# Update and norm between two stages by halves of the tokens, in a two-layer diffusion block on one core

## The reference

```python
def rms_norm(x, g):
    y = xf * lax.rsqrt(jnp.mean(xf * xf, axis=-1, keepdims=True) + EPS)
def modulate(x, g, shift, scale):
    return rms_norm(x, g) * (1.0 + scale) + shift
def swiglu(u, wg, wu, wd):
    return (jax.nn.silu(u @ wg) * (u @ wu)) @ wd
def ffn_sublayer(x, shift, scale, gate, g_pre, g_post, wg, wu, wd):
    y = swiglu(modulate(x, g_pre, shift, scale), wg, wu, wd)
    return x + FFN_RES * gate * rms_norm(y, g_post)
...
h = ffn_sublayer(h, ...); hc = ffn_sublayer(hc, ...)                # latent, context
y, yc = token_mixing(modulate(h, ...), modulate(hc, ...), ...)      # w_in 1024 x 2608, attention, gla, mLSTM, w_out
h = h + mod[:, 5] * rms_norm(y, g[3])
h = ffn_sublayer(h, ...)
if need_ctx: hc = ...                                               # not in the last layer
```

## Time and profile before

| | us |
|---|---|
| median of 3 runs | 1999.89 (1999.27 to 2004.18) |
| profiled execution | 2008.94 |
| its span, first to last instruction | 2007.1 |
| PE busy in it | 1873.5 (93%) |
| DVE busy | 1109.3 (55%) |
| ACT busy | 760.1 (38%) |
| POOL busy | 243.6 (12%) |

### The profile page before, as it was taken

One profiled execution on the slowest core, in us unless ns is written; L12 is line 12 of the kernel. 1 busy time (PEld: TensorE's weight loads), 2 busy tenths in 40 slices (PEclk: granted clock), 3 DMA queues, 4 the chain that ended last, 5 costly groups with the idle time before them and its releaser, 6 DMA issues. The chain is left out here.

```text
span 2007.1 us, 25666 instructions
## 1 busy us (share of the span) xinstructions
PE 1873.5 (93%) x10461; PEld 1521.9 (76%) x10461; DVE 1109.3 (55%) x1630; ACT 760.1 (38%) x1132; POOL 243.6 (12%) x327
## 2 busy tenths in 40 slices
PE   5999999979998886999999979999999799879998
PEld 3788877857786664888778858887888488769997
DVE  1777722245756646777522267775222676855544
ACT  4423222236436445222313253222232645654443
POOL 4011110012531000111110001110000152000000
PEclk7999999989999797999999979999999799979999
DMA  9566654342321022666553416665234243036654
...
DMA packets 366469, 254.05 MB, mean 127 GB/s; under 512 B 30610, under 2 KB 343276, under 8 KB 366352
## 3 DMA queue, kind: packets, MB, share of 16 engines
...
...
## 5 line engine op out<-in xcount | busy, mean ns | idle before, releaser
L324 PE MATMUL bank<-u_hi,w_hi 128*128 128x512 f32 (+2 forms) x1872 | 690.8, 369 | 29.7 <-DVE u_lo L1000 20.6
L325 PE MATMUL bank<-u_lo,w_hi 128*128 128x512 f32 (+2 forms) x1872 | 682.8, 365 | 0.0
L326 PE MATMUL bank<-u_hi,w_lo 128*128 128x512 f32 (+2 forms) x1872 | 682.5, 365 | 0.0
L308 DVE TENSOR_TENSOR w_lo<-raw,w_hi 128x2048 fp32r<-128x2048 f32 (+2 forms) x182 | 373.0, 2049 | 262.3 <-ACT w_hi L300 262.1
L324 PEld LDWEIGHTS bank<-u_hi,w_hi 128*128 128x128 f32 (+1 forms) x1872 | 357.8, 191 | 110.8 <-issue 51.6
L326 PEld LDWEIGHTS bank<-u_hi,w_lo 128*128 128x128 f32 (+1 forms) x1872 | 357.5, 191 | 56.8 <-issue 0.9
L325 PEld LDWEIGHTS bank<-u_lo,w_hi 128*128 128x128 f32 (+1 forms) x1872 | 358.1, 191 | 53.8 <-issue 0.5
L300 ACT ACTIVATE w_hi<-raw 128x2048 fp32r<-128x2048 f32 (+2 forms) x182 | 311.8, 1713 | 144.0 <-PE bank L326 126.6
L324 PE MATMUL bank<-ht_hi,w_hi 128*128 128x512 f32 (+1 forms) x704 | 256.8, 365 | 1.4 <-DVE w_lo L308 1.4
L326 PE MATMUL bank<-ht_hi,w_lo 128*128 128x512 f32 (+1 forms) x704 | 255.3, 363 | 0.0
L325 PE MATMUL bank<-ht_lo,w_hi 128*128 128x512 f32 (+1 forms) x704 | 255.2, 363 | 0.0
...
## 6 DMA issues: line engine op xcount, KB each, us to landing
ada_slot<-in_ada_w_dram POOLq DMA_DIRECT2D x128, 512.0 KB, 4.7
...
```

Of the source, the lines that this page charges most:

```text
L308: nc.vector.tensor_tensor(w_lo[s][:, 0:size], raw[s][:, 0:size], w_hi[s][:, 0:size].bitcast(F32), ALU.subtract).then_inc(lo_ready[s], 1)
L324: nc.tensor.matmul(acc, wh, xh, start=first, stop=False)
L325: nc.tensor.matmul(acc, wh, xl, start=False, stop=False)
L326: return nc.tensor.matmul(acc, wl, xh, start=False, stop=last)
```

## The change

For the four boundaries after z = 0 to 3 (`HALVED = 4`), everything between two stages is done for the first 256 tokens and then for the second 256. Boundaries z = 4 and the end stay as they are. `posts` and `norms` give the new counts of passes for the semaphores.

- The last output tile is made in two halves of 256 columns in two banks; both its weight units are held until the second half has used them. In the down stage its second unit is split right after tile 6 instead of after tile 6's squares and copies, and the next stage's first unit is split later, after the second square of the update.
- Sums and spreads take four strips of 64 tokens for a half. They stand between the products of the last tile's second half and of the next stage's first two units.
- The next stage's first two units (four tiles) are done for the first half of the tokens, then for the second half. In the projection tiles 0 to 3 have banks of their own, and `gla_after(2)` and `(3)` come after tile 3.
- DVE mixes the norm of the first half with the update of the second half.

```diff
+HALF = (slice(0, LAT), slice(LAT, TOK))
+LAST_BANKS, POST_SUMS, NORM_BANKS = (5, 6), 7, (4, 7)
+STRIP = LAT // 4
...
+    def last_half(dst, z, h):
+        acc = bank[LAST_BANKS[h]][:, HALF[h]]
+        nc.scalar.activation(tmp_a[1][:, HALF[h]], acc, ACT.Square).then_inc(post["ysq_ready"], 1)
+        nc.scalar.activation(dst[:, KT - 1, HALF[h]], acc, ACT.Copy,
+                             scale=mod[z // 3][:, 3 * (z % 3) + 2, KT - 1, h:h + 1]).then_inc(post["y_ready"], 1)
+    def half_root(sums, h, of_norm, need, ready, need_count):
+        act.wait_ge(need, need_count)
+        nc.scalar.activation(rstd_part(h, of_norm), bank[sums][:, 0:STRIP], ACT.Sqrt, bias=eps_col[:],
+                             scale=1.0 / DM).then_inc(ready, 1)
+    def half_square(z, h, k):
+        act.wait_ge(post["h_added"], KT * posts(z, h) + k + 1)
+        if h + k > 0:
+            wait(act, norm["sq_used"], KT * norms(z + 1, h) + k - 1)
+        nc.scalar.activation(tmp_a[k % 2][:, HALF[h]], H[:, k, HALF[h]], ACT.Square).then_inc(norm["sq_ready"], 1)
+    def half_mod(z, h, k):
+        layer, q = (z + 1) // 3, (z + 1) % 3
+        part = tmp_b[k % 2][:, HALF[h]]
+        at = KT * norms(z + 1, h) + k + 1
+        act.wait_ge(norm["scaled"], at)
+        nc.scalar.activation(part, part, ACT.Identity, bias=mod[layer][:, 3 * q, k, h:h + 1],
+                             scale=mod[layer][:, 3 * q + 1, k, h:h + 1]).then_inc(norm["moded"], 1)
+        act.wait_ge(norm["moded"], at)
+        nc.scalar.activation(u_hi[:, k, HALF[h]], part, ACT.Copy).then_inc(norm["uhi_ready"], 1)
+    def halved_norm(z, Y, n_last):
+        layer, q = (z + 1) // 3, (z + 1) % 3
+        act.wait_ge(post["ysq_added"], (KT - 1) * z + KT - 2)
+        act.wait_ge(post["lat_done"], z + 1)
+        last_half(Y, z, 0)
+        half_root(POST_SUMS, 0, 0, post["ss_done"], post["ss_rms"], posts(z) + 1)
+        if z == 1:
+            unit_done(act, n_last, 0, 2, 0)
+            last_half(Y, z, 1)
+        for k in range(KT):
+            if z != 1 and k == 2:
+                split_hi(act, second_unit(layer, q) - 1)
+            if z == 1 and k == KT // 2:
+                split_hi(act, second_unit(layer, q))
+            half_square(z, 0, k)
+        if z != 1:
+            unit_done(act, n_last, 0, 2, 0)
+            last_half(Y, z, 1)
+        half_root(NORM_BANKS[0], 0, 1, norm["sq_used"], norm["rms_ready"], KT * norms(z + 1) + KT)
+        half_root(POST_SUMS, 1, 0, post["ss_done"], post["ss_rms"], posts(z, 1) + 1)
+        if z != 1:
+            split_hi(act, second_unit(layer, q))
+        for k in range(KT):
+            half_mod(z, 0, k)
+            if k >= KT // 2:
+                half_square(z, 1, k - KT // 2)
+        for k in range(KT // 2, KT):
+            half_square(z, 1, k)
+        half_root(NORM_BANKS[1], 1, 1, norm["sq_used"], norm["rms_ready"], KT * norms(z + 1, 1) + KT)
+        for k in range(KT):
+            half_mod(z, 1, k)
...
+                if z < HALVED and 2 * i + t == KT - 1:
+                    halved_norm(z, Y_ffn, n0 + 2 * KT - 1)
+                else:
+                    unit_done(act, n0, i, 4, 2 * t + 1)
+                    if z < HALVED and 2 * i + t == KT - 2:
+                        split_hi(act, n0 + 2 * KT - 1)
+                    post_tile(Y_ffn, z, 2 * i + t, t, T)
...
+            if z < HALVED and t == KT - 1:
+                halved_norm(z, Y_mix, n0 + t // 2)
+                return
+            if z < HALVED and t == KT - 2:
+                act.wait_ge(post["six_done"], 1)
+            else:
...
+        dve.wait_ge(need, need_count)
+        nc.vector.reciprocal(rstd_part(h, of_norm), rstd_part(h, of_norm)).then_inc(ready, 1)
+    def halved_norm(z, Y):
+        layer, q = (z + 1) // 3, (z + 1) % 3
+        def y_scale(h, k):
+            if h + k > 0:
+                wait(dve, post["h_added"], KT * posts(z, h) + k - 1)
+            nc.vector.tensor_tensor(tmp_b[k % 2][:, HALF[h]], Y[:, k, HALF[h]], bank[LAST_BANKS[h]][:, HALF[h]], ALU.mult)\
+                .then_inc(post["y_scaled"], 1)
+        def h_add(h, k):
+            dve.wait_ge(post["y_scaled"], KT * posts(z, h) + k + 1)
+            nc.vector.tensor_tensor(H[:, k, HALF[h]], H[:, k, HALF[h]], tmp_b[k % 2][:, HALF[h]], ALU.add)\
+                .then_inc(post["h_added"], 1)
+        def u_scale(h, k):
+            if k >= 2:
+                dve.wait_ge(norm["u_ready"], KT * norms(z + 1, h) + k - 1)
+            nc.vector.tensor_tensor(tmp_b[k % 2][:, HALF[h]], H[:, k, HALF[h]], bank[NORM_BANKS[h]][:, HALF[h]], ALU.mult)\
+                .then_inc(norm["scaled"], 1)
+        def low(h, k):
+            dve.wait_ge(norm["uhi_ready"], KT * norms(z + 1, h) + k + 1)
+            nc.vector.tensor_tensor(u_lo[:, k, HALF[h]], tmp_b[k % 2][:, HALF[h]], u_hi[:, k, HALF[h]].bitcast(F32),
+                                    ALU.subtract).then_inc(norm["u_ready"], 1)
+        half_invert(0, 0, post["ss_rms"], posts(z) + 1, post["ss_rstd"])
+        dve.wait_ge(mod_done, max(MODS_BEFORE_POST[z], MODS_BEFORE[z + 1]))
+        dve.wait_ge(post["ss_spread"], posts(z) + 1)
+        y_scale(0, 0)
+        for k in range(KT):
+            if k + 1 < KT:
+                y_scale(0, k + 1)
+            h_add(0, k)
+        split_lo(dve, second_unit(layer, q) - (1 if z != 1 else 0))
+        half_invert(0, 1, norm["rms_ready"], norms(z + 1) + 1, norm["rstd_ready"])
+        dve.wait_ge(norm["rstd_spread"], norms(z + 1) + 1)
+        for k in range(KT):
+            u_scale(0, k)
+            if k == 1:
+                half_invert(1, 0, post["ss_rms"], posts(z, 1) + 1, post["ss_rstd"])
+            if k == 2:
+                dve.wait_ge(post["ss_spread"], posts(z, 1) + 1)
+            if k >= 1:
+                low(0, k - 1)
+            if k >= 2:
+                y_scale(1, k - 2)
+            if k >= 3:
+                h_add(1, k - 3)
+        low(0, KT - 1)
+        if z != 1:
+            split_lo(dve, second_unit(layer, q))
+        y_scale(1, KT - 2)
+        h_add(1, KT - 3)
+        y_scale(1, KT - 1)
+        h_add(1, KT - 2)
+        h_add(1, KT - 1)
+        half_invert(1, 1, norm["rms_ready"], norms(z + 1, 1) + 1, norm["rstd_ready"])
+        dve.wait_ge(norm["rstd_spread"], norms(z + 1, 1) + 1)
+        for k in range(KT):
+            u_scale(1, k)
+            if k >= 1:
+                low(1, k - 1)
+        low(1, KT - 1)
...
+    def half_sums(sums, squares, h, first, last):
+        for g in range(4):
+            at = h * LAT + g * STRIP
+            ins = nc.tensor.matmul(bank[sums][32 * g:32 * g + 32, 0:STRIP], ones[:].to_broadcast([P, 32]), squares[:, at:at + STRIP],
+                                   start=first, stop=last)
+        return ins
...
+    def half_spread(to, h, of_norm):
+        for g in range(4):
+            at = h * LAT + g * STRIP
+            ins = nc.tensor.matmul(bank[to][:, at:at + STRIP], ident[:, 32 * g:32 * g + 1].to_broadcast([P, P]),
+                                   rstd_part(h, of_norm), start=True, stop=True)
+        return ins
+    def post_sums(z, h):
+        if h == 0:
+            pe.wait_ge(post["ysq_added"], (KT - 1) * (z + 1))
+        half_sums(POST_SUMS, sq_sum, h, True, False)
+        pe.wait_ge(post["ysq_ready"], KT * (z + 1) + z + h)
+        half_sums(POST_SUMS, tmp_a[1], h, False, True).then_inc(post["ss_done"], 1)
...
+        begin(n0)
+        wait(pe, gated["prod_ready"], FT * g)
+        for k in range(KT):
+            u_part(z, 0, k)
+            for w in range(2):
+                part(0, w, k, 0)
+            if k == 0:
+                post_spread(z - 1, 1)
+            if k >= 4:
+                norm_sum(z - 1, 1, k - 4)
+        begin(n0 + 1)
+        for w in range(2):
+            for k in range(KT):
+                part(1, w, k, 0)
+                n = w * KT + k
+                if n in (0, 2, 4, 6):
+                    norm_sum(z - 1, 1, n // 2 + 4)
+                if n == 11:
+                    norm_spread(z - 1, 1)
+        for k in range(KT):
+            u_part(z, 1, k)
+            for w in range(2):
+                last = part(0, w, k, 1)
+        last.then_inc(unit_used[n0 % 2], 1)
+        for w in range(2):
+            for k in range(KT):
+                last = part(1, w, k, 1)
+        last.then_inc(unit_used[(n0 + 1) % 2], 1)
...
+        def last_tile():
+            for h in range(2):
+                for f in range(FT):
+                    s, k = (n0 + f // half) % 2, f % half
+                    if h == 0 and k == 0:
+                        begin(n0 + 2 * KT - 2 + f // half)
+                    if h == 1 and f == 2:
+                        post_sums(z, 0)
+                    if h == 1 and f == 6:
+                        post_spread(z, 0)
+                    if h == 1 and f in (15, 20):
+                        norm_sum(z, 0, f // 20)
```

(62 more changed lines are left out.)

152 lines of the change are left out of this document (103 added, 49 removed).

## The result

The changed kernel takes 2010.53 us (median of 9 runs), the kernel before 2004.18 us in the same session: ratio 1.004, 95% interval 1.0022 to 1.0058. It is slower, by 4 to 12 us. The forecast was 6.6 us slower (2006.5 from the 1999.9 of the three earlier runs of before); the median of before lay 4.3 us higher this time, and so did the time after.

A forecast was written before the change was run, and what follows sets the result against it. The DVE, ACT, PE chain at the stage boundaries, not PE, was taken as the limit. Terms -0.9, -1.9 - 1.5, +1.2 - 1.5 and -2.0 made 6.6 us slower, 2006.5 us from 1999.9; range 1989 to 2019.

The forecast's parts named there:

- Last tile: Last output tile before a down boundary, made in halves with inserted sums and spread: ends at 17.8 us instead of 15.0.
- k = 1: Second k step of the next stage's first pass: begins only at 29.4 us, behind the second half's spread of 1.9.
- Steps of k: Next stage's first pass over k: four DVE operations of 0.34 make 1.36 us per k for 0.72 of products.
- rival D: DVE operations chained by semaphores start 0.42 us apart, not 0.33: 8 us more, 2014.5 us; chance 0.06.
- Second unit: Next stage's second weight unit: DVE's split ends at 39.3 us and PE waits 1.2 us for it.
- Second pass: Second half of the next stage's first two tiles: ACT's pace of 1.0 us per k; all four tiles done at 61.5.
- z = 1 and 2: Boundaries after output projection (z = 1) and down projection (z = 2): loss 1.9 us, gain 1.2 us, without later stalls.
- Third unit: Third weight unit of the gate-up stage (z = 1, 2), not split before the first is used: stall 1.5 us, twice.
- gla: Gated linear attention chain, starting behind tiles 2 and 3: loss 0.9 us at z = 0, 2.0 at z = 3.
- Rival A: PE stays at 2.4 GHz through the shorter pause and inserts cost half: together 12.8 us, 1993.7 us, faster; chance 0.27.
- Rival B: Covers behind the boundary hold (gla level 1, third unit): 1998.2 us, no change; chance 0.20.
- Rival C: The paced stretch keeps PE at 1.2 GHz into the ahead tiles: 14 us more, 2020 us; chance 0.08.

The follow-up runs named there:

- e1: Changed kernel with the second half's post-norm reciprocal and spread moved into the pause, behind the first half's norm spread; ratio 0.9974 against the kernel before.
- e2: Changed kernel with the third weight unit split on ACT before the first silu and on DVE before the first product; ratio 1.0025 against the kernel before.
- e5: Changed kernel with added unneeded products in the pause of three down boundaries, to hold PE's clock; ratio 1.0065 against the kernel before.

## Why the prediction held, step by step

I take t = 0 at 412.3, the start of the last tile at z = 0 after the change.

- **Last tile.** Predicted end 17.8 for 15.0, measured 18.1. The inserts of 0.3: the sum at 429.37 stands where the next product, due 0.12 behind that of 429.16, comes at 429.61, so 0.33. The spread at the upper clock took 1.00 for 1.1.
- **First product.** 25.7 said, 438.10 is 25.8. At z = 1: 20.3 said, 20.4.
- **k = 1.** 29.4 said, 441.70 is 29.4. The spread of 64 columns, which I took at 1.9 at the lower clock between bounds of 0.5 and 2.1, lasted 1.80 to 1.97. At the upper clock it took 1.00 (1.1 said), where the whole one of before took 1.16 (z = 3), so a half costs a little less than a whole. This was the largest unknown, and e1 shows what hung on its place: 2.3 us at k = 1 and 3.0 and 3.1 over the stretches of z = 1 and 2, since VectorE's low half 1 and all behind it waited for it.
- **Steps of k.** 1.36 said, 1.33 measured. VectorE's operations started 0.33 apart, so rival D was wrong.
- **Second unit.** Wait 1.2 said at 39.3; 1.02 at 39.1.
- **Second pass.** 1.0 per k said, four tiles done at 61.5; L2066 is at 61.9. At z = 3 it was said at 60.7 and came at 61.5.
- **z = 1 and 2.** Here part of the match is luck. I put the sums of 759.88 at the end of the last tile of z = 1, t = 5.4; they are at 7.0, since PE idles 1.42 in front of them. So the four tiles of before end at 54.4 and not at 53.0, those of after at 56.0 and not at 54.9, and two errors leave a loss of 1.6 for 1.9. At z = 2 the pause was 0.7 shorter than I had it (25.0 for 25.7), its first spread being at the upper clock, and the four tiles took 36.5 for 35.8: they end at 61.5 as said.
- **Third unit.** 1.5 said, 1.37 measured, twice. What I did not see is that the fourth is as late (e2): the price of the edit is VectorE's sums in front of all of them, not the order of one split.
- **gla.** At z = 3 level 1 was said at 91.3 and came at 91.1, but only because a start 0.8 late was made good by 29.7 from there for the 30.6 that I had. At z = 0 it was said at 93.6 and came at 95.0, and this is the one term of the sum that was mis-sized: 0.9 said, 2.3 measured. Of the 1.4, 0.4 is L2066's start; for the rest I had the exp follow POOL's exponents at once. The exponents were ready 19.25 us behind L2066, as in before, but the exp started 1.4 later, behind the table load of 1.28. In the kernel before that load stood at 491.94, under a wait for PE's tiles.
- **Sum.** -6.6 said; the stretches give -7.6, the interval of the ratio -4.4 to -11.6. The waits came where I had put them; that the total came so close owes something to errors that cancel.

Rival A (PE stays at 2.4 GHz) was wrong at z = 0, 1 and 3, where the first spread in the pause took 1.87 to 1.97. Its inserts cost 0.33 and not half. At z = 2 the first spread took 1.10 and the pause was 7.0, as at 16 of the 24 down boundaries of the kernels with strips of 64 and no added products: the first spread starts 3.78 us behind the last product at all of them and takes 1.10 to 1.97 alone, 2.00 to 3.68 with the second behind it. So the fall comes before it, in it or behind it, and 0.9 us hang on that. e5 put a price on the clock, 0.9 at the first spread, 0.8 at the second and 0.6 in the six products, 2.2 a boundary, which is what I had computed for A, but it can't be had by products that stand between the sums. Rival B failed on both covers. Rival C: the clock was back some 6 us after the first product, at 444.3, and the ahead tiles ran at 0.12.

What I left out was an order that was free to take. I priced the second spread between k = 0 and 1 at 1.9 and did not ask whether it could stand in the pause, where PE waited 2.15 us for the first low half.
